# A recurrent layer whose weight blocks are split by two engines instead of one

## The reference

```python
q = silu(xn @ w_q); z = xn @ w_f; v = xn @ w_i
logf = logaddexp(log1p(-lb) + log_sigmoid(z), log(max(lb, 1e-30)));  k = (1 - lb) * sigmoid(-z)
S_t = diag(f_t) S_{t-1} + k_t v_t^T,   o_t = S_t^T q_t         # exact, blockwise
out = (rmsnorm(o) * silu(xn @ w_g)) @ w_o
```

## Time and profile before

| | |
|---|---|
| median of 3 runs | 3007.53 us (3007.15 to 3008.85) |
| the profiled execution | 3012.8 us, of which the span from first to last instruction is 3011.0 us |
| PE busy | 2858.0 us, 95% of the span |
| DVE busy | 1326.1 us, 44% |
| POOL busy | 790.8 us, 26% |
| ACT busy | 516.1 us, 17% |
| mean granted TensorE clock | 0.983 of full speed |

### The profile page before, as it was taken

One profiled execution on the slowest core, in us unless ns is written; L12 is line 12 of the kernel. 1 busy time (PEld: TensorE's weight loads), 2 busy tenths in 40 slices (PEclk: granted clock), 3 DMA queues, 4 the chain that ended last, 5 costly groups with the idle time before them and its releaser, 6 DMA issues. The chain is left out here.

```text
span 3011.0 us, 51347 instructions
## 1 busy us (share of the span) xinstructions
PE 2858.0 (95%) x21758; PEld 2712.4 (90%) x21758; DVE 1326.1 (44%) x1721; ACT 516.1 (17%) x827; POOL 790.8 (26%) x465
## 2 busy tenths in 40 slices
PE   6999999988999999999998999899999999999998
PEld 6988888887999999999987999766799999999997
DVE  6555555554633332333455666355454223332333
ACT  3122222221200000000113444333211000000001
POOL 2211111112333333333331110012133333333331
PEclk8999999999999999999999999999999999999999
DMA  4111111121111111111111001366211111111111
GB/s 109 51 52 52 52 52 52 43 75 36 48 44 49 43 43 50 43 50 42 43 45 38 30 30 35 128 254 260 65 49 43 50 43 48 44 43 50 43 50 71
DMA packets 211388, 183.92 MB, mean 61 GB/s; under 512 B 21776, under 2 KB 199232, under 8 KB 209120
## 3 DMA queue, kind: packets, MB, share of 16 engines
q1 hardware_dynamic: 175808, 123.58, 13.6%
q0 software_dynamic: 4608, 41.95, 3.6%
q10 hardware_dynamic: 30752, 14.99, 1.9%
HBM read 162.79 MB, written 17.71 MB: 60 GB/s over the span
## 5 line engine op out<-in xcount | busy, mean ns | idle before, releaser
L164 POOL CAST w_hi<-w_raw 128x1024 fp32r<-128x1024 f32 (+3 forms) x190 | 188.0, 989 | 1782.5 <-PEq L1136 1514.5
L166 POOL TENSOR_TENSOR w_lo<-w_raw,w_hi 128x1024 fp32r<-128x1024 f32 (+3 forms) x190 | 497.2, 2617 | 15.2
L217 PE MATMUL G<-xg_lo_a,w_hi 128*128 128x350 f32 (+1 forms) x1788 | 418.4, 336 | 43.0 <-DVE xg_lo_a L279 20.2
L217 PE MATMUL G<-xg_hi_a,w_hi 128*128 128x350 f32 (+1 forms) x1788 | 398.7, 325 | 0.0
L217 PE MATMUL G<-xg_hi_a,w_lo 128*128 128x350 f32 (+1 forms) x1788 | 398.2, 325 | 0.0
L1334 DVE TENSOR_TENSOR h<-h,G 128x1050 f32<-128x1050 f32 x120 | 149.8, 1248 | 482.6 <-PE G L217 482.6
L217 PEld LDWEIGHTS G<-xg_lo_a,w_hi 128*128 128x128 f32 (+1 forms) x1788 | 303.6, 190 | 61.7 <-issue 32.4
L217 PE MATMUL G<-a_lo,w_hi 128*128 128x350 f32 x1536 | 331.1, 323 | 0.0
L217 PE MATMUL G<-a_hi,w_hi 128*128 128x350 f32 x1536 | 330.9, 324 | 0.0
L217 PE MATMUL G<-a_hi,w_lo 128*128 128x350 f32 x1536 | 330.1, 323 | 0.0
L217 PEld LDWEIGHTS G<-xg_hi_a,w_lo 128*128 128x128 f32 (+1 forms) x1788 | 307.9, 190 | 1.2
(11 more groups left out here) (386 smaller groups left out, 3751.9 us busy)
## 6 DMA issues: line engine op xcount, KB each, us to landing
w_raw<-in_w_up SPq DMA_DIRECT2D x64, 512.0 KB, 4.1
w_raw<-in_w_down SPq DMA_DIRECT2D x64, 512.0 KB, 3.4
w_raw<-in_hg_wq SPq DMA_DIRECT2D x8, 512.0 KB, 3.9
w_raw<-in_hg_wf SPq DMA_DIRECT2D x8, 512.0 KB, 3.8
w_raw<-in_hg_wi SPq DMA_DIRECT2D x8, 512.0 KB, 3.8
w_raw<-in_hg_wg SPq DMA_DIRECT2D x8, 512.0 KB, 6.0
s_old<-in_state_hgrn ACTq DMA_DIRECT2D x8, 512.0 KB, 4.6
out_state_hgrn_sample<-s_new ACTq DMA_DIRECT2D x8, 512.0 KB, 3.4
```

The lines of the kernel that those rows point to most:

```text
L164: nc.gpsimd.tensor_copy(high, raw).then_inc(k.w_hi_done, 1)
L166: nc.gpsimd.tensor_tensor(low, raw, high, ALU.subtract).then_inc(k.w_split, 1)
L217: last = nc.tensor.matmul(out, w(a, t), x(b, t, c), start=(t == 0 and (a, b) == ORDER[0]), stop=(t == nk - 1 and (a, b) == ORDER[-1]))
```

## The change

For the blocks of heads 1 to 7 (apart from the very first of head 1) and for the first block of the output projection, POOL does only the cast (`cast_block`), and DVE does the subtraction (`weight_low`), four times in each of the 7 iterations: behind the recurrence work of slots 1, 5, 8 and 12. The blocks 0 to 4 and the later ones of the output projection are split by POOL as before, in code that is written out instead of a loop.

```diff
+def cast_block(k, pool, n, width):
+    slot = n % 2
+    pool.wait_ge(k.w_loaded[slot], (n // 2 + 1) * 16)
+    pool.wait_ge(k.w_used, n + 1)
+    k.nc.gpsimd.tensor_copy(k.w_hi[:, slot, 0:width], k.w_raw[:, slot, 0:width]).then_inc(k.w_hi_done, 1)
...
+LOW_AT = (1, 5, 8, 12)
...
             @block.gpsimd
             def _(pool):
-                split_blocks(k, pool, 4 * HEADS)
-                split_blocks(k, pool, KD, (n_early * P, n_early * P), first=4 * HEADS)
-                split_blocks(k, pool, 2, (4 * P, 4 * P), first=4 * HEADS + KD)
+                for n in range(5):
+                    split_block(k, pool, w0 + n, WB)
+                for n in range(5, 4 * HEADS):
+                    cast_block(k, pool, w0 + n, WB)
+                cast_block(k, pool, w0 + 4 * HEADS, n_early * P)
+                for n in range(1, KD):
+                    split_block(k, pool, w0 + 4 * HEADS + n, n_early * P)
...
+                def weight_low(h, j):
+                    dve.wait_ge(k.w_hi_done, h * 4 + w0 + 4 + j + 1)
+                    nc.vector.tensor_tensor(k.w_lo[:, j % 2, :], k.w_raw[:, j % 2, :], k.w_hi[:, j % 2, :],
+                                            ALU.subtract).then_inc(k.w_split, 1)
+
                 def both(h):
                     for slot in range(SLOTS):
                         rec(h, slot)
+                        if slot in LOW_AT:
+                            weight_low(h, LOW_AT.index(slot) + 1)
                         if slot == 3:
                             take(h, 3)
```

More of the change, by code:

```diff
@@ L544, in _ @@
             def _(pool):
-                split_blocks(k, pool, 4 * HEADS)
-                split_blocks(k, pool, KD, (n_early * P, n_early * P), first=4 * HEADS)
-                split_blocks(k, pool, 2, (4 * P, 4 * P), first=4 * HEADS + KD)
+                for n in range(5):
[5 more added lines that the diff above has]
+                    split_block(k, pool, w0 + 4 * HEADS + n, n_early * P)
+                for n in range(2):
+                    split_block(k, pool, w0 + 4 * HEADS + KD + n, 4 * P)
             @block.tensor
```

## The result

The changed kernel takes 2972.27 us (median of 4 runs, 2970.04 to 2977.39) where the kernel before took 3007.34 (4 runs, 2992.62 to 3008.85). The ratio is 0.9891, with a 95% interval from 0.9872 to 0.9910: some 33 us faster. In a later session with the kernel before beside it (7 runs against 26) the changed kernel came to 0.9922 (0.9896 to 0.9948), and single runs of either spread over 15 to 26 us. What spreads them is part of the answer.

The account below looks back on a forecast made before the run. PE was taken to bound the loop, waiting on DVE's count of `level`; -13.3 + 0.6 = -12.7 us from the profiled 3012.8 gave 3000.1, scaled to the median 2995 us, range 2990 to 3002.

Parts of the forecast that it names:

- The bound and the cause: PE bounds the loop; POOL's subtraction in slot 4 slows L999, so PE waits 1.90 us for `level` in 7 iterations.
- The added subtraction in slot 5: On DVE in slot 5: takes 1.22 us and makes PE wait 0.08 us at slot 7, 0.6 us in all.
- The rival of the slow subtraction: Slot 5's added subtraction takes 2.2 us, PE waits at slot 7, only 5.9 us won: 3001.6 us; chance 0.15.
- The other three subtractions cost nothing: DVE's added work in slots 1, 8 and 12 is covered by its own waiting, at least 1.7 us (slot 8).
- The slower rival: Slot 8's wait for the cast blocks DVE and delays `s_new` for PE: 3013.5 us or more; chance 0.06.
- The moved loads: Loads released later in slots 1 and 5: no cast late, PE's "issue" waits changed by 0, 3.5 us kept either side.
- the main term: PE's waits on `level` ahead of slot 5 go whole: 7 x 1.90 = 13.3 us won.
- The bound of 3.5 us: Allowance for changed "issue" waits of PE in the loop: half a us per iteration, on either side.
- The price of a wait: Each PE wait on `level` ahead of slot 5 was counted at its own length, 1.90 us, seven times.
- the 0.6 us taken off for slot 7: PE's new wait at slot 7's score block behind the added subtraction: 7 x 0.08 us, subtracted from the gain.

Follow-up runs that it names:

- only_slot1: Changed kernel, but DVE subtracts only the block of slot 1 and POOL the others, slot 4's included: 2996.55 us, ratio 0.9970.
- slot0: Changed kernel with the first of DVE's four subtractions behind slot 0 instead of slot 1: 2980.24 us, ratio 0.9934.
- only_slot5: Changed kernel, but DVE subtracts only the block of slot 5 and POOL the other three: 2974.33 us, ratio 0.9923.

## Why the prediction was wrong

*The bound and the cause.* Right. PE's waits on `level` came from POOL's subtraction meeting L999; with the subtraction gone L999 takes 0.69 us (forecast 0.70) and all of the 13.3 us are gone. only_slot1, which leaves that subtraction to POOL, keeps 13.2 us.

*The added subtraction in slot 5.* Right: 1.22 to 1.23 us in all 28 (forecast 1.22), and the score block of slot 7 shows no wait (forecast 0.08 us each). The rival of the slow subtraction fell with that. The lock that the Trainium skill states ("SBUF — State Buffer", section "Who interferes with whom") agrees with both: the operation was slow beside POOL's subtraction, and takes its short time without it.

*The other three subtractions cost nothing.* Right on DVE: the wait for the cast in slot 8 delayed nobody, PE has no wait on `s_new` in the loop. The slower rival fell.

*The moved loads, with PE's "issue" waits taken as 0.* This is the step that failed: "Unknown is what the shifted loads and the shorter slot do to PE's "issue" waits ... I take 0 and keep half a us per iteration ... on either side". In the two profiles it was worth 13.4 us, as much as the main term. The rows held more of it than the prediction used: one line of "issue" waits out of two was looked at, and its wait was put down to code that was not touched. But the wait is a transfer. The shifted load ended the wait in slot 2 (only_slot1 and slot0 show that from two sides). Of that line's 8.3 us 4.3 lie in iterations 1 to 3, where both kernels fetched, and are the shift's; 0.7 lie in iteration 0; and 3.2 lie in iterations 4 to 6, where the changed kernel fetched nothing, so they would have gone without the shift too. The returns that fetched nothing bring 5.1 us more. The bound of 3.5 us should have been the 19.0 us of the two lines, on the side of a gain.

*The price of a wait.* A second term was too small even where no code is fetched: the change is worth 17.3 us there, not 12.7. The prediction priced each wait at its own length; three of seven cost 1.5 us more through the lower clock behind them (4.5 us), and the 0.6 us taken off for slot 7 did not come. In the two profiles of the result this has no part: each has one stretch at the lower clock in the loop, behind a return.

*The rest.* 6.3 us of the difference of the two profiles lie behind the loop, and they do not go with the change. From the first step behind the loop to the end it is 2396.0 us before and 2389.7 after, but 2389.2 in the kernel before with the shorter loop and 2390.0 in the changed one with it.

*What stays open.* Why the changed kernel's loop finds its code in place in more of its returns than the kernel before does. 240 counts or 28 instructions fewer ended the fetches, 128 counts brought them in every iteration, so its branch lies near a border where a further block is fetched; that between the two it is a race, which small differences in time can turn, is argued and not shown. In the profiles the kernel before fetched in 6 of 6 iterations, the changed one in 3 of 6 and 0 of 6, only_slot5 in 0 of 6, only_slot1 and slot0 in 5 of 6. No run singles out what turned it, and the gain of about 33 us, or 23 us in the second session, holds for such a mix.

## What to carry to other kernels

An "issue" wait of PE in a loop is to be looked up in the instruction queue of the DMA list: if packets come in each iteration, the time hangs on other transfers and on where the loop's branch lies, and a loop that is a few instructions shorter can be worth nearly as much as the change under study (here 3002.40 to 2986.78, 15.6 us, against 17.3). Two variants that differ in such a way are compared fairly only once their loops fetch nothing; here the shorter loop turned a spread of over 20 us in the kernel before into one of 6 (5 in the changed one), and the change's own gain (17.3 us) could be read. A two-input operation on DVE is checked for what POOL does in the same microseconds, and a load that is released later or earlier for every transfer that it then stands in front of.

## What was not expected of the hardware

Three of seven waits of TensorE of some 1.8 us in one profile were followed by a stretch at mostly the lower level of its clock, 1.5 us each; after the other four it stayed high, and in the kernel before after all seven. The code of a loop with some 1700 multiplications and weight loads can stay in place over six iterations without one fetch, and leaving out 28 instructions was enough to make it so. A count of a semaphore on PE is not free: 112 more of them (240 against 128) lengthened PE's idle time ahead of a product from 22.2 to 39.4 us, by estimate 0.15 us each. The first 128 put the loop only 2 to 3 us back, because PE waited for data there anyway.
